# An MLA and pooling encoder block on one core: gate sums behind the third pool group, pair 1's weight sums on DVE, down-weight sums later

## The reference

```
h = rmsnorm(x, g_mix) * (1 + sc1) + sh1
proj = h @ w_in                                  # q latent 256, kv latent 128, rope key 64, pool 512
y_mla = mla_mixer(...)                           # 4 heads, chunk-causal, queries and values through the latent
y_pool = pool_mixer(proj[..., o3:], w_pool, pool_scale)   # trailing means over 2, 4, 8, 16, one w_pool per group
x = x + gt1 * (concat(y_mla, y_pool) @ w_o)
h = rmsnorm(x, g_ffn) * (1 + sc2) + sh2
x = x + gt2 * ((silu(h @ w_gate) * (h @ w_up)) @ w_down)
return rmsnorm(x, g_final)
```

## Time and profile before

| | |
|---|---|
| median of 3 runs | 1072.49 us (1072.03 to 1076.76) |
| the profiled execution's own time | 1072.65 us |
| its span | 1070.6 us |
| PE busy | 997.6 us, 93% |
| DVE, ACT, POOL busy | 682.7, 446.0, 341.5 us |
| DMA engines, mean | 45.6% of 16 engines' span, 154 GB/s |
| chain that ended last | PE 66%, DVE 15%, DMA 5%, issue 5%, ACT 4%, POOL 3% |

### The profile page before, as it was taken

One profiled execution on the slowest core, in us unless ns is written; L12 is line 12 of the kernel. 1 busy time (PEld: TensorE's weight loads), 2 busy tenths in 40 slices (PEclk: granted clock), 3 DMA queues, 4 the chain that ended last, 5 costly groups with the idle time before them and its releaser, 6 DMA issues.

```text
span 1070.6 us, 12560 instructions
## 1 busy us (share of the span) xinstructions
PE 997.6 (93%) x4605; PEld 816.5 (76%) x4605; DVE 682.7 (64%) x985; ACT 446.0 (42%) x759; POOL 341.5 (32%) x250
## 2 busy tenths in 40 slices
PE   5799699999998799968999999999999999999996
PEld 1698486788887687856888888888888888878884
DVE  5839845767528789865356347437536737748777
ACT  1671147877620176623324333332433514544432
POOL 1213657005012021445434533633453000028510
PEclk9699799999999899988999999999999999999998
DMA  9903200201046525244662573465365878955613
GB/s 331 336 11 108 60 1 1 79 1 46 34 142 229 180 80 157 89 163 142 187 194 93 174 216 114 123 216 159 107 187 193 310 254 302 366 170 184 216 59 158
DMA packets 119544, 165.19 MB, mean 154 GB/s; under 512 B 8310, under 2 KB 61370, under 8 KB 119484
## 3 DMA queue, kind: packets, MB, share of 16 engines
q1 hardware_dynamic: 119484, 164.39, 45.6%
HBM read 124.26 MB, written 40.11 MB: 154 GB/s over the span
## 4 chain that ended last, share of the span: by engine, by line
PE 66%; DVE 15%; DMA 5%; issue 5%; ACT 4%; POOL 3%; SPq 2%; DVEq 0%; POOLq 0%; ACTq 0%
PE PS L2096 34%; PE PS L2130 15%; PE PS L1802 11%; DMA ADA<-in_w_ada 3%; PE PS L1976 2%; PE PS L1861 2%; DVE ACC L1278 2%; DVE GT L1278 2%; DMA REraw<-t_scratch 1%; DVE RS L1254 1%; PE PS L1988 1%; DMA W12raw<-in_w_up 1%; POOL ropeQ L725 1%; ACT PR L968 1%; DVE WO1lo L1290 1%
## 5 line engine op out<-in xcount | busy, mean ns | idle before, releaser
L2130 PE MATMUL PS<-RE 128*128 128x512 f32 x924 | 210.5, 390 | 1.4 <-ACT DU L1194 1.4
L2130 PEld LDWEIGHTS PS<-RE 128*128 128x128 f32 x924 | 173.4, 188 | 38.2 <-ACT DU L1194 1.8
L1290 DVE TENSOR_TENSOR RE<-REraw,RE 128x1024 fp32r<-128x1024 f32 x77 | 105.7, 1409 | 76.2 <-ACT RE L1129 74.7
L2096 PE MATMUL PS<-HB,WS 128*128 128x512 f32 x528 | 124.7, 392 | 9.8 <-ACT PV L1112 9.8
L2096 PE MATMUL PS<-HT,WS 128*128 128x512 f32 x528 | 125.8, 395 | 3.6 <-ACT PV L1112 3.6
L1129 ACT ACTIVATE RE<-REraw 128x1024 fp32r<-128x1024 f32 x77 | 80.6, 1061 | 106.2 <-DMA REraw<-in_w_down 55.4
L2096 PEld LDWEIGHTS PS<-HB,WS 128*128 128x128 f32 x528 | 100.0, 190 | 31.1 <-issue 10.2
L2096 PEld LDWEIGHTS PS<-HT,WS 128*128 128x128 f32 x528 | 100.8, 191 | 25.2 <-issue 4.0
L2096 PE MATMUL PS<-HT,W 128*128 128x512 f32 x480 | 112.4, 393 | 0.0
L2096 PEld LDWEIGHTS PS<-HT,W 128*128 128x128 f32 x480 | 91.1, 190 | 19.3 <-DVE W L1290 0.3
L1656 DVE TENSOR_TENSOR SG<-PS,PV 128x512 f32<-128x512 f32 x22 | 15.2, 691 | 122.0 <-PE PS L2096 104.6
(11 more groups left out here) (252 smaller groups left out, 1808.1 us busy)
## 6 DMA issues: line engine op xcount, KB each, us to landing
ADA<-in_w_ada SPq DMA_DIRECT2D x20, 1024.0 KB, 7.0
REraw<-h_scratch SPq DMA_DIRECT2D x77, 256.0 KB, 4.8
h_scratch<-SG SPq DMA_DIRECT2D x55, 256.0 KB, 2.4
TW<-in_w_down SPq DMA_DIRECT2D x22, 512.0 KB, 4.6
t_scratch<-TW SPq DMA_DIRECT2D x44, 256.0 KB, 2.9
REraw<-t_scratch SPq DMA_DIRECT2D x44, 256.0 KB, 6.2
REraw<-in_w_down SPq DMA_DIRECT2D x33, 256.0 KB, 5.3
X<-in_x SPq DMA_DIRECT2D x16, 512.0 KB, 11.7
```

The lines of the kernel that those rows point to most:

```text
L1290: dve.tensor_tensor(out_, full, hi.bitcast(F32), ALU.subtract).then_inc(ready, 1)
L2096: ins = pe.matmul(PS[:, bank, :], l, r, start=fresh and z == 0, stop=z == len(terms) - 1, skip_group_check=not fresh)
L2130: ins = pe.matmul(PS[:, D_BASE[p] + j, :], RE[e][:, a, 0, tok(j)], RE[e][:, b, 1, :], start=p in (1, 2, 7) and i == 0 and x_ == 0, stop=i ...
```

## The change

Seven edits in two places.

First place: PE does `col_sum(2)`, `col_sum(3)` after `pool_group(2)` and the second four transposes, and the transposes of WUK after `pool_group(3)`. DVE's `accumulate(6)` and `(7)` move behind `lt_lo(3)` (7 behind the splits of WP and WUV), `wu_lo(3)` between them, `gate(0)`, `gate(1)` behind the last `lt_lo`. SP loads WUraw(3) at `u_done` 4, ahead of the wait for `acc_done` 8. POOL's `wu_hi(3)` moves to between the second and the third window sum of the first group. ACT does WUQ and `u_out(3)` before WUK.

Second place: pair 1's four weight sums leave POOL for DVE (`w_sum_second`), where each needs the same stages as before; pair 1's subtractions go 6, 5, 7, 3, 4, and DVE does 6 and 5 ahead of `mul_h(0, 1)`. POOL's `tw_sums(0)` now waits for `prod` after (1, 6, 1), and from pair 1 on `w_sums(pair + 1)` stands ahead of `tw_sums(pair)`, where it stood behind it.

```diff
--- before.py
+++ after.py
@@ -355,7 +355,7 @@
             return HB[:, part, {6: 0, 7: 1, 4: 2}[p], k, :]
         return HT[:, part, k + (HK if p in (2, 3) else 0), half(1 if p in (3, 5) else 0)]
 
-    LO_ORDER = [(1, 2, 6, 5, 4, 7, 3), (5, 7, 6, 3, 4)] + [(5, 7, 1, 6, 3, 2, 4)] * (NC - 2)
+    LO_ORDER = [(1, 2, 6, 5, 4, 7, 3), (6, 5, 7, 3, 4)] + [(5, 7, 1, 6, 3, 2, 4)] * (NC - 2)
     HI_ORDER = [(6, 5, 4, 7, 3), (5, 6, 7, 3, 4)] + [(1, 5, 6, 7, 3, 4)] * (NC - 2)
 
     def count(orders, n, p):
@@ -459,11 +459,11 @@
         sp.wait_ge(S["u_done"], 2)
         load_wu(2)
 
+        sp.wait_ge(S["u_done"], 4)
+        load_wu(3)
         sp.wait_ge(S["acc_done"], 8)
         sp.dma_start(WUQraw[:], wuq_d).then_inc(S["wuq_in"], 16)
         sp.dma_start(WUKraw[:], w_uk.rearrange("l c h d -> c (l h) d")).then_inc(S["wuk_in"], 16)
-        sp.wait_ge(S["u_done"], 4)
-        load_wu(3)
 
         sp.wait_ge(S["ql_done"], 8)
         for i in range(4):
@@ -707,12 +707,12 @@
 
                 then(pool.tensor_tensor(dst[:, PADW:], src[:, PADW:], src[:, PADW - 2 ** s:PADW + SEQ - 2 ** s], ALU.add))
                 src, dst = dst, WIN[:, (s + 1) % 2]
+                if i == 0 and s == 1:
+                    wu_hi(3)
 
             w = 2 ** (g + 1)
             then(pool.tensor_tensor(src[:, PADW:PADW + w], src[:, PADW:PADW + w], INV[:, 0:w], ALU.mult))
             pool.tensor_scalar(src[:, PADW:PADW + w], src[:, PADW:PADW + w], float(w), 0.0, ALU.mult, ALU.add).then_inc(S["windowed"], 1)
-            if i == 0:
-                wu_hi(3)
             pool.wait_ge(S["pooled"], i + 1)
 
         def rotate(i, t):
@@ -803,12 +803,12 @@
         w12_first_hi()
         h2_hi(3)
         w_sums_first()
-        w_sums(1)
-        tw_sums(0)
-        for pair in range(1, NC):
+        for pair in range(NC):
+            if 1 <= pair < NC - 1:
+                w_sums(pair + 1)
+            if pair == 0:
+                pool.wait_ge(S["prod"], after(1, 6, 1))
             tw_sums(pair)
-            if pair < NC - 1:
-                w_sums(pair + 1)
 
         pool.wait_ge(S["tw_out"], 64 * NC)
         pool.memset(GT2[:], 0.0).then_inc(S["gt_zero"], 1)
@@ -910,12 +910,12 @@
         for t in range(4, NT):
             lt_hi(t)
 
-        act.wait_ge(S["wukT"], 1)
-        act.activation(WUK[:, HI].rearrange("p h c -> p (h c)"), PS[:, 6, :], ACT.Copy).then_inc(S["wuk_hi"], 1)
         act.wait_ge(S["wuq_in"], 16)
         act.activation(WUQ[:, HI].rearrange("p k h d -> p (k h d)"), WUQraw[:].rearrange("p k h d -> p (k h d)"),
                        ACT.Copy).then_inc(S["wuq_hi"], 1)
         u_out(3)
+        act.wait_ge(S["wukT"], 1)
+        act.activation(WUK[:, HI].rearrange("p h c -> p (h c)"), PS[:, 6, :], ACT.Copy).then_inc(S["wuk_hi"], 1)
 
         for i, t in enumerate(BLOCKS):
             act.wait_ge(S["qr_done"], i + 1)
@@ -1380,8 +1380,6 @@
                                      ALU.mult, ALU.mult).then_inc(S["tm_norm"], 1)
         dve.wait_ge(S["ckv_hi"], 1)
         lo(CKV[:, LO], TMO[:, :, QR:QR + LAT], CKV[:, HI], S["ckv_ready"])
-        accumulate(6)
-        accumulate(7)
 
         def lt_lo(t):
             dve.wait_ge(S["lt_hi"], t + 1)
@@ -1403,18 +1401,20 @@
         wu_lo(2)
         lt_lo(2)
         lt_lo(3)
+        accumulate(6)
+        wu_lo(3)
         dve.wait_ge(S["wp_hi"], 1)
         lo(flat(WP[:, LO]), flat(WPraw[:]), flat(WP[:, HI]), S["wp_ready"])
         dve.wait_ge(S["wuv_hi"], 1)
         lo(flat(WUV[:, LO]), flat(WUVraw[:]), flat(WUV[:, HI]), S["wuv_ready"])
-        gate(0)
-        gate(1)
-        wu_lo(3)
+        accumulate(7)
         pooled(0)
         for t in range(4, NT):
             lt_lo(t)
             if t == 5:
                 pooled(1)
+        gate(0)
+        gate(1)
         dve.wait_ge(S["wuq_hi"], 1)
         lo(WUQ[:, LO].rearrange("p k h d -> p (k h d)"), WUQraw[:].rearrange("p k h d -> p (k h d)"),
            WUQ[:, HI].rearrange("p k h d -> p (k h d)"), S["wuq_ready"])
@@ -1593,6 +1593,24 @@
             if t >= 2:
                 dve.wait_ge(S["t2"], t - 1)
             dve.tensor_scalar(XN[:, t % 2], X[:, t, :], RS2[:, t:t + 1], None, ALU.mult).then_inc(S["xn2"], 1)
+
+        def w_sum_second(p):
+            r = W12raw[:, LO]
+            if p == 5:
+                dve.wait_ge(S["prod"], after(0, 5, 1))
+                dve.wait_ge(S["w34_in"], 64)
+                dve.tensor_tensor(WSf[:, SLOT[5], LO], W34raw[:, :, 0:HK], W34raw[:, :, HK:KT], ALU.add).then_inc(S["w_sum"], 1)
+            elif p == 6:
+                dve.wait_ge(S["w_sum"], 5)
+                dve.wait_ge(S["w12_in"], 32)
+                dve.tensor_tensor(WSf[:, SLOT[6], LO], WSf[:, SLOT[5], LO], r[:, :, 0:HK], ALU.subtract).then_inc(S["w_sum"], 1)
+            elif p == 7:
+                dve.wait_ge(S["prod"], after(0, 7, 1))
+                dve.tensor_tensor(WSf[:, SLOT[7], LO], r[:, :, 0:HK], W34raw[:, :, 0:HK], ALU.subtract).then_inc(S["w_sum"], 1)
+            else:
+                dve.wait_ge(S["prod"], after(0, 3, 1))
+                dve.wait_ge(S["w_sum"], 6)
+                dve.tensor_tensor(WSf[:, SLOT[3], LO], r[:, :, HK:KT], WSf[:, SLOT[6], LO], ALU.subtract).then_inc(S["w_sum"], 1)
 
         def w_lo(n, *slots):
 
@@ -1699,15 +1717,19 @@
         w_lo(0, 3)
         mul_h(0, 0)
         part_lo(9, HT[:, LO, HK:KT, half(1)], HTf[:, HK:KT, half(1)], HT[:, HI, HK:KT, half(1)])
+        w_sum_second(5)
+        w_sum_second(6)
         add_c(0, 3, 0)
         part_lo(10, HB[:, LO, 2], HBf[:, LO, 2], HB[:, HI, 2])
         add_c(0, 3, 1)
+        w_sum_second(7)
+        mul_h(0, 3)
+        w_sum_second(3)
+        w_lo(1, 6)
         w_lo(1, 5)
-        mul_h(0, 3)
-        w_lo(1, 7)
         mul_h(0, 1)
         h_sums(0)
-        w_lo(1, 6)
+        w_lo(1, 7)
         add_c(0, 2, 0)
         w_lo(1, 3)
         add_c(0, 2, 1)
@@ -1884,17 +1906,17 @@
         pool_group(1)
         for t in range(4):
             turn_latents(t)
-        col_sum(2)
-        col_sum(3)
         pool_group(2)
         for t in range(4, NT):
             turn_latents(t)
+        col_sum(2)
+        col_sum(3)
+        pool_group(3)
         pe.wait_ge(S["wuk_in"], 16)
         pe.wait_ge(S["gt_ready"], 2)
         for h in range(HEADS):
             ins = pe.transpose(PS[:, 6, h * P:(h + 1) * P], WUKraw[:, h, :], IDENT[:])
         ins.then_inc(S["wukT"], 1)
-        pool_group(3)
 
 
         pe.wait_ge(S["wuq_ready"], 1)
```

## The result

The changed kernel takes **1099.1 us** (median of four runs, 1097.39 to 1100.82), the kernel before 1074.33 beside it (1072.03 to 1076.76): a ratio of 1.023, 95% interval 1.020 to 1.026. The forecast was 1105, slower. The profiled execution has a span of 1099.0 us against 1070.6. It was the slowest of the four (1100.82 us), so its 28.4 us of span stand against 24.8 us between the medians. PE's waits, as before: engine, line waited for, us in total, times, longest.

A forecast was written before the change was run, and what follows sets the result against it. PE was taken as the bound nearly everywhere. 1072.65 - 6.4 (first place) + 6.0 (second place) + 21.2 (waits in nine pairs) + 11.9 (clock) = 1105.35, so 1105 us; range 1084 to 1112, held at about 0.8.

The forecast's parts named there:

- First place: Up to the rotations: PE's wait for the gate sums goes, third pool group 8.6 us earlier; -6.4 us.
- Second place: Feed-forward: (1, 6) starts 5.1 us earlier, but later loads start (1, 3) later; +6.0 us net, the 5.1 already spent.
- Both bounds: For the gate-sum stretch: -9.4 us, the whole wait, and -4 if WUQ's split or a held `pooled` ends last.
- One of my signs of being wrong: W12 of pair 2 landing by 490; the other such sign was no wait in pairs 2 to 10.
- The 8.8 us: Estimate for three 1 MiB loads at about 358 GB/s, not 13.1 us; (1, 3) would then cost +1.7.
- Nine pairs: Pairs 2 to 10: four additions take turns with DVE, delaying the W12 split past 1.3 us slack; 9 x 2.35 = 21.2 us.
- The forecast's chain: Around pair 4: POOL and DVE alternate instructions, so the W12 split ends at 588.5 and PE waits 2.35 us.
- The clock: Behind the waits in pairs 2 to 10: a fall to 1.2 GHz costs 1.7 us, on seven of nine; 11.9 us.
- what shifts on DVE behind the split costs nothing: In the pairs: DVE's other work shifts by 3 us at no cost, since it feeds stages 10 us or more away.
- Rivals 2 and 3: DVE held under 1.3 us, nine pairs free: 1072 us (0.09); the same with loads of 9 us: 1068 us (0.07).
- Rival 4: Pairs 2 to 10 stall but the clock never falls there: 1093 us; counted within the main forecast's 0.84.
- my main line: Stalls in nine pairs, with the clock falling behind seven: 1105 us, 1088 to 1112 as a case, chance 0.84.

The follow-up runs named there:

- d3_three: The changed kernel with three down-weight additions in place of four in pairs 1 to 9 (the third left out): 1091.11 us, ratio 1.016.

## Why the prediction was right, and where it was off

**First place: forecast -6.4, measured -8.2 in the trace and -8.7 in its own run.** The order of events was as worked out; with the 0.85 by which this trace starts late, the eight additions are done at 130.6 (131.6 forecast), the fourth group starts at 133.2 (135.2), and the rotations at 152.4 (160.14 in the earlier trace rows). Up to PE's first query product the trace shows 6.9 us (160.16 against 167.01), 7.7 by the kernel's own clock. The other 1.3 of the 8.2 come up to 454, in stretches that the change doesn't touch, and I put them down to no term; (0, 4) was 7.8 earlier in the first place's own trace. Two terms were too dear: POOL's window additions ahead of the split were priced at the 2.42 us of the earlier trace rows, though nothing on DVE held the first ones any more (1.89 each), and the two column sums took 1.3 us together, not 2. Both bounds held.

**Second place: forecast -5.1 and +6.0 net, measured -4.9 (4.92 of idle time against 9.81) and +5.5.** `load_tw(1)` came at 473.69, which is 481.9 without the first place's gain (481.4 forecast); from there (1, 3) took 14.7 us, not 15.7. From `load_tw(1)` to ACT's start on W12 at 485.86 it was 12.2 us. One of my signs of being wrong, W12 of pair 2 landing by 490, came true by its words; it was written without the first place's gain. With the 8.2 put back, W12 lands at 494.1, and my own forecast for that clock was 494.6. The 8.8 us estimated from the Trainium skill (SBUF — State Buffer, Summary: rules for kernel authors) are not seen here either.

**Nine pairs: forecast 9 x 2.35 = 21.2, measured 22.8.** The mechanism is shown three ways: it appears alone with the loop's order, goes with it, and grows with the number of additions. The delay of the split was as forecast: DVE's rows last 1.09, 0.97, 1.09 and 0.51 longer than alone, 3.66 in all, against 588.5 - 584.83 = 3.67. The 1.6 more are mostly the restart, which I had left out: from (n, 2) to the next stage PE takes 5.57 us in place of 5.44 behind each wait, 9 x 0.13 = 1.2. The rule of the exclusive lock (Trainium skill: SBUF — State Buffer, Who interferes with whom) agrees with the trace for pairs of SBUF operands: 1.66 to 2.17 us where 0.69 is the work alone. The same page (Trainium skill: SBUF — State Buffer, SBUF: two separate sides) limits the lock on DVE's side to operations with two SBUF inputs and to a fast mode that uses two ports; the addition with an operand in PSUM, 0.68 us beside POOL's fourth, agrees. The forecast's chain gave that addition no time of its own, so there the fourth addition cost about half a microsecond net, as it does in the trace. It was the later expectations for three and two additions that charged every one at 1.16.

**The clock: the term that was mis-sized.** I charged 1.7 us at seven of nine waits, 11.9 in all, from one row with 2.12 us of idle time. The price was about right (1.55 us), the count was two, so 3.1. The step that failed is "I charge it on seven of nine", which took the fall from the idle time's length: the length alone doesn't decide (below).

**Left out: 4.1 us at (10, 4) and 2.2 in the down projection.** I had written that what shifts on DVE behind the split costs nothing, and had not followed SP. In the nine pairs its queue is held until the additions end, which costs nothing there. At the last pair it does, by the timelines: TW(10) is asked for only at 840.56, its sums are sent away at 853.11, and transfers of the down projection's weights stand behind them, from 855.00, 3.5 us ahead of (10, 3) where it was 7.5 before (828.94 and 836.40); ACT and DVE get them late, and the `add_c` for (10, 4) waits on DVE behind their splits. That chain was not tried by itself, so it is argued and not shown; with two, three and five additions in the pairs the same wait is 2.8, 1.0 and 1.2 us. The loop's new order alone has the same wait (2.3), the old loop has none.

**The sum.** Errors: -1.8 first place, -0.5 and -1.1 second place, +1.6 waits, -8.8 clock, +6.3 left out, together -4.3, which is 1099.0 against the 1103.3 of span in the forecast. The two largest nearly cancel, so the closeness of the number is in part luck. The range held the time; its low end took -8.4 and +2 for the two places, where the bounds beside them were -9.4 and +1.2, so by its own bounds it would have been 1082. Rivals 2 and 3 needed DVE to be held for less than 1.3 us; it was 3.7 (1.33 of slack, 2.24 of idle time, 0.16 of overlap). Rival 4, no fall of the clock at 1093, was nearer than my main line in its clock term.

## What to carry to other kernels

When an engine's queue is reordered inside a loop, look not at what the moved work needs but at what the other engines do in the moment it now runs: four short additions per pair that made PE wait nowhere in their old place cost 32 us in the new one, against a slack of 1.3 us that no wait in the profile before showed. Price each part of a change by itself: two parts worth 8.7 and 4.4 us were buried under two edits in one loop, and 1060.6 us was to be had. Before a step is postponed, follow the DMA queue that sends its result away, since everything behind it in that queue is postponed too.

## What the runs showed of the hardware

**The same idle time, two clocks.** Around the waits of 2.22 and 2.25 us shown above, in windows of 4 us (sum, PE busy, granted clock, DMA share, GB/s):

```profile
504.80:508.80 4.00, 1.78 (x8) 0.94 0.41 153
508.80:512.80 4.00, 4.00 (x12) 0.63 1.03 382
...
546.90:550.90 4.00, 1.75 (x8) 1.00 0.42 155
550.90:554.90 4.00, 4.00 (x19) 1.00 1.03 381
```

Behind the first, PE ran a part at 1.2 GHz, behind the second all at 2.4 GHz, with the same work around both. In the profiled execution of the changed kernel the two falls among the nine come at 508.58 and 713.14, without the wait for (1, 6, 1) at 499.96 and 704.65: the same two waits each time, those of pairs 2 and 7. With five additions every second wait has one, and length doesn't order them:

```profile
510.30 7.36 PE L2120 MATMUL PS<-HT,W 128*128 128x512 f32 x24 [3.07 <-DVE W L1292]
...
553.61 5.74 PE L2120 MATMUL PS<-HT,W 128*128 128x512 f32 x24 [3.31 <-DVE W L1292]
```

3.07 us of idle time cost the clock, 3.31 didn't. With waits of up to 1.74 us none of the 18 at (n, 2) had a fall. PE's wait for ACT's DU, in the down projection, shows the same: behind 1.98 us (above) the clock fell and a row took 10.06 us, behind 2.48 it did not (`d3_three`):

```profile
956.87 8.47 PE L2153 MATMUL PS<-RE 128*128 128x512 f32 x36 [2.48 <-ACT DU L1195]
```

So for the idle times of 2.0 to 3.3 us seen here the length alone doesn't say whether the clock falls; something else, such as the moment at which PE stands idle, decides as well. The Trainium skill (TensorE: Matmul & The Clock Gate, What's actually happening) says that the chip judges PE's activity in windows that run on by themselves and don't start anew with a kernel. The trace agrees as far as it goes: equal idle times, other moments, other clocks. That the same two pairs had the falls in two kernels, whose waits of pair 2 ended 8.6 us apart, is not explained by that. What sets the moment was not tested and stays open.
